# HGRN's eight projection blocks beside the forget ones as seven half products, with in-place quarter sums on GpSimd

## What is computed

```python
(hq, hf, hi, hg, gq, gk, gv, ga, gb, gz, gate_h, gate_g) = jnp.split(u @ w_in, offsets, axis=-1)
log_f = jnp.logaddexp(jnp.log(lb), jnp.log1p(-lb) + jax.nn.log_sigmoid(hf))
k_h = -jnp.expm1(log_f)
q_h = jax.nn.silu(hq) * HG_DK ** -0.5
o_h = hgrn2_chunked(q_h, k_h, hi, log_f)          # 8 heads of 128, chunks of 64
o_h = rmsnorm(o_h, hgrn_out_norm) * jax.nn.silu(hg)
y_h = o_h @ w_branch_hgrn
y = jax.nn.sigmoid(gate_h) * y_h + jax.nn.sigmoid(gate_g) * y_g
```

## Time and profile before

| | us |
|---|---|
| median of three runs | 2774.72 |
| lowest and highest | 2771.5, 2782.12 |
| profiled execution, whole | 2772.54 |
| its span | 2770.7 |
| from the start of hf to the start of y_h | 1189.6 to 1560.1 |

### The profile page before, as it was taken

The page is one execution under the profiler, slowest core; times in us unless marked ns, Lnnn a source line. Parts: engine busy times, 40 slices in busy tenths (PEclk is TensorE's granted clock), DMA queues, the critical chain, the costliest instruction groups (busy, mean ns, idle before and its releaser), DMA issues.

```text
span 2770.7 us, 29212 instructions
## 1 busy us (share of the span) xinstructions
PE 2708.6 (98%) x11644; PEld 1812.8 (65%) x11644; DVE 1260.6 (45%) x2499; ACT 638.8 (23%) x1460; POOL 59.6 (2%) x115
## 2 busy tenths in 40 slices
PE   8999899999999999999999999999999999999999
PEld 5445557656468888746556655656565685688886
DVE  3823333445234445526354426474655451344564
ACT  2122321246210000133342222424243202100001
POOL 0000000000000000000000001010110000000000
PEclk9999899999999999999999999999999999999999
DMA  4111011200122222211110130121111321222222
GB/s 157 61 61 58 25 57 66 91 31 1 61 64 89 91 92 91 77 61 61 61 61 31 63 122 31 61 77 40 68 46 61 145 91 61 91 92 85 74 86 76
DMA packets 122479, 195.17 MB, mean 70 GB/s; under 512 B 7212, under 2 KB 63336, under 8 KB 121448
## 3 DMA queue, kind: packets, MB, share of 16 engines
q1 hardware_dynamic: 120784, 181.15, 19.2%
q0 software_dynamic: 1296, 12.06, 1.1%
q10 hardware_dynamic: 264, 0.10, 0.0%
HBM read 185.95 MB, written 7.34 MB: 70 GB/s over the span
## 4 chain that ended last, share of the span: by engine, by line
PE 95%; DVE 2%; ACT 1%; DMA 1%; issue 1%; ACTq 0%; DVEq 0%; SPq 0%
PE psum L506 19%; PE psum L503 14%; PE psum L2239 14%; PE psum L416 9%; PE psum L436 8%; PE psum L2221 7%; PE psum L401 6%; PE psum L1141 2%; PE psum L2102 2%; PE psum L1161 2%; PE psum L634 1%; PE psum L389 1%; PE psum L1149 1%; PE psum L2450 1%; PE psum L2316 1%
## 5 line engine op out<-in xcount | busy, mean ns | idle before, releaser
L2239 PE MATMUL psum<-weight_ring,h_t 128*128 128x512 f32 x896 | 406.6, 596 | 0.5 <-issue 0.5
L559 DVE TENSOR_TENSOR arena<-arena,psum 128x512 f32<-128x512 f32 x179 | 122.9, 686 | 336.8 <-PE psum L506 287.6
L2239 PEld LDWEIGHTS psum<-weight_ring,h_t 128*128 128x128 f32 x896 | 162.0, 191 | 162.3 <-issue 161.1
L416 PE MATMUL psum<-h_t,weight_ring 128*128 128x512 f32 x560 | 245.7, 599 | 7.9 <-DMA weight_ring<-in_w_in_dram 4.2
L2221 PE MATMUL psum<-h_t,weight_ring 128*128 128x512 f32 x512 | 235.4, 601 | 1.7 <-ACT arena L2623 1.4
L506 PE MATMUL psum<-h_t,weight_ring 128*128 128x256 f32 x1024 | 228.2, 379 | 0.0
L503 PE MATMUL psum<-weight_ring,arena 128*128 128x256 f32 x992 | 220.2, 379 | 1.5 <-ACT arena L2660 1.5
L506 PEld LDWEIGHTS psum<-h_t,weight_ring 128*128 128x128 f32 x1024 | 194.5, 190 | 27.5 <-issue 1.3
L503 PEld LDWEIGHTS psum<-weight_ring,arena 128*128 128x128 f32 x992 | 188.4, 190 | 27.7 <-issue 2.2
L416 PEld LDWEIGHTS psum<-h_t,weight_ring 128*128 128x128 f32 x560 | 106.9, 192 | 142.3 <-issue 133.8
L401 PE MATMUL psum<-weight_ring,h_t 128*128 128x512 f32 (+3 forms) x512 | 182.1, 512 | 0.8 <-DVEq L1587 0.8
(11 more groups left out here) (396 smaller groups left out, 3288.6 us busy)
## 6 DMA issues: line engine op xcount, KB each, us to landing
weight_ring<-in_ffn_w_in_dram SPq DMA_DIRECT2D x44, 1024.0 KB, 7.3
weight_ring<-in_w_in_dram SPq DMA_DIRECT2D x20, 2048.0 KB, 7.8
weight_ring<-in_ffn_w_out_dram SPq DMA_DIRECT2D x8, 2048.0 KB, 8.0
weight_ring<-in_w_in_even_dram SPq DMA_DIRECT2D x7, 2048.0 KB, 8.1
weight_ring<-in_w_in_odd_dram SPq DMA_DIRECT2D x5, 2048.0 KB, 7.8
weight_ring<-in_w_in_dram SPq DMA_DIRECT2D x8, 1024.0 KB, 7.0
weight_ring<-in_w_branch_gdn_dram SPq DMA_DIRECT2D x4, 2048.0 KB, 7.9
weight_ring<-in_ffn_w_out_dram SPq DMA_DIRECT2D x4, 1536.0 KB, 6.7
```

The source lines that it names most:

```text
L416: last = pe.matmul(bank, slot[:, k, c:c + P], act[:, k, :], start=(k == 0), stop=(k == KD - 1))
L559: ins = dve.tensor_tensor(out, other, bank, op)
L2239: last = pe.matmul(bank, act[:, k, t * P:(t + 1) * P], slot[:, k, :], start=(k == 0), stop=(k == KD - 1))
```

## The change

Eight blocks, all but hf's, become seven half products each (`pe_seven_streamed`), in the order p4, p1, p2, p5, p6, p7, p3. It is a generator: `pe_take(stream, 1)` does one half product, 8 matmuls, so that they can stand between heads. The weights' sums are made by GpSimd in the ring itself (`pool_quarter_sums`): four operations of 128x1024 a block, the first after p4 has used the quarter that it overwrites, the third after p1, the fourth after p2; TensorE waits for the first at p5, for the third at p6, for the fourth at p3. The sums of the activations are made once, by VectorE, into the buffer of the residual `x_res`, which GpSimd's queue has written out to a scratch tensor in HBM and reads back after gate_h 1 (2 MB each way). Of a block's results ScalarE copies p4 (negated), p1 and p5, three operations of 128x512, and VectorE adds the rest in seven (`dve_streamed`). The activations Silu and Sigmoid, before taken from PSUM with the copy, are now applied to the finished blocks in SBUF. `HGRN_UNITS` says how many half products stand ahead of the first level and after each of them: 4, then 2, 2, 2, 2, 1, 1, 0 for half 0 and 6, then 2, 2, 2, 1, 1, 0, 0 for half 1.

```diff
+STREAMED = ("p4", "p1", "p2", "p5", "p6", "p7", "p3")
+def pe_seven_streamed(K, pe, key, act, tokens, token_major, among=None):
+    blk = K.next_block()
...
+    t1, t2, t4, t3 = sums_view(tokens, KD)
+    sides = {"p4": (w22, t4), "p1": (w11, x11), "p2": (w12, x21), "p5": (w22, t1), "p6": (w11, t2), "p7": (w21, t3),
+             "p3": (w12, x22)}
+    summed = {"p5": 1, "p6": 3, "p7": 3, "p3": 4}
...
+    for name in STREAMED:
...
+        if K.turn((key, name)) > 1:
+            pe.wait_ge(K.free_of((key, name)), K.turn((key, name)) - 1)
+        if name in summed:
+            pe.wait_ge(K.quarters_summed, at + summed[name])
...
+        yield
+def pool_quarter_sums(K, pool, key, blk):
+    w11, w12, w21, w22 = quarters(K, blk, KD)
+    pool.wait_ge(K.full_of((key, "p4")), K.turn((key, "p4")))
+    pool.tensor_tensor(w22, w21, w22, ALU.add).then_inc(K.quarters_summed, 1)
...
+    pool.tensor_tensor(w21, w11, w21, ALU.subtract).then_inc(K.quarters_summed, 1)
+    pool.wait_ge(K.full_of((key, "p1")), K.turn((key, "p1")))
...
+    pool.tensor_tensor(w11, w22, w11, ALU.subtract).then_inc(K.quarters_summed, 1)
+    pool.wait_ge(K.full_of((key, "p2")), K.turn((key, "p2")))
...
+    pool.tensor_tensor(w12, w12, w11, ALU.subtract).then_inc(K.quarters_summed, 1)
+def dve_streamed(K, dve, key, name, quarter, base, tmp):
...
+    if name == "p6":
+        dve_product(K, dve, key, "p6", base, base)
+        dve.wait_ge(K.free_of((key, "p5")), K.turn((key, "p5")))
+        dve.tensor_tensor(c12, pair(base), pair(tmp), ALU.add).then_inc(K.one_more("dve"), 1)
...
@@ pe_mix
+    K.token_sums["pe"] += 1
+    pe.wait_ge(K.tokens_summed, K.token_sums["pe"])
+    pe_take(pe_seven_streamed(K, pe, (s, "hq", 0), K.h_t, V["tokens_s"], False), 7)
     for g in range(2):
...
+        inner = pe_hgrn_stream(K, pe, s, V, g)
+        pe_take(inner, HGRN_UNITS[g][0])
...
+            pe_take(inner, HGRN_UNITS[g][1][lv])
...
-        pe_take(fill, 2 * KD)
+        pe_take(fill, 2)
         pe.wait_ge(K.phase_met, K.phase_end("pe"))
+        pe_take(fill, 2)
         pe_hgrn_states(K, pe, s, V, g, fill)
...
-            pe_take(fill, 2 * KD)
+            fill = pe_seven_streamed(K, pe, (s, "gate_h", 1), K.h_t, V["tokens_s"], True, FILL_BANKS)
+            pe_take(fill, 2)
         pe.wait_ge(K.phase_met, K.phase_end("pe"))
+    pe_take(fill, 2)
     pe.wait_ge(K.hgrn_gated, 2)
...
-    pe_take(fill, 2 * KD)
+    pe_take(fill, 3)
...
+HGRN_UNITS = ((4, (2, 2, 2, 2, 1, 1, 0)), (6, (2, 2, 2, 1, 1, 0, 0)))
...
@@ pe_hgrn_states
         if h == 3:
-            pe_take(fill, KD)
+            pe_take(fill, 2)
...
-    pe_take(fill, KD)
+    pe_take(fill, 1)
     pe.wait_ge(K.hgrn_states, g + 1)
...
@@ act_mix
+        part(beside, "p4")
+        part(beside, "p1")
         act.wait_ge(K.hgrn_to_end, g + 1)
...
@@ dve_mix
+    dve.wait_ge(K.x_spilled, 16)
+    dve_token_sums(K, dve, K.h_t, KD, V["tokens_s"])
...
+        dve.wait_ge(K.gates_open, g + 1)
         dve_head_norm(K, dve, V["o"], g * 512, 128, V["gate"], K.hgrn_squares, g + 1,
...
+    dve_hgrn_sums(K, dve, s, V, "gate_h", 1, ("p6", "p7"))
+    dve_weight_sums(K, dve, K.branch_blocks["y_h"], KD, V["weights0"], None)
+    dve_hgrn_sums(K, dve, s, V, "gate_h", 1, ("p3",))
+    dve_weight_sums(K, dve, K.branch_blocks["y_h"] + 1, KD, V["weights1"], None)
...
+def pool_hgrn(K, pool, s):
+    pool.wait_ge(K.lb_shifted, 1)
+    pool.dma_start(K.x_dram, K.x_res[:]).then_inc(K.x_spilled, 16)
+    for name, g in HGRN_ORDER:
+        pool_quarter_sums(K, pool, (s, name, g), K.streamed_at[(name, g)])
...
+    pool.dma_start(K.x_res[:], K.x_dram).then_inc(K.x_reloaded, 16)
```

More of the change, by code:

```diff
@@ L2531, in act_mix @@
         act.wait_ge(K.free_of((s, "o_t", kt)), K.turn((s, "o_t", kt)))
-    act_gate(K, act, V["gate_y"], (s, "gate_h", 1), 1, (2, 3))
+    for half in range(2):
+        last = ((s, "gate_h", half), "p3")
+        act.wait_ge(K.free_of(last), K.turn(last))
+        gate = V["gate_y"][:, :, half * BANK:(half + 1) * BANK]
+        act.activation(gate, gate, ACT.Sigmoid).then_inc(K.gates_open, 1)
     for half in range(2):
@@ L2906, in dve_mix @@
         dve_seven_fresh(K, dve, (s, "y_h", half), quarter, V["base"][:, 0, :])
[L2907 to L2908 removed]
+        dve.wait_ge(K.gates_open, 3 + half)
         y, gate = (V[name][:, :, half * BANK:(half + 1) * BANK] for name in ("y", "gate_y"))
```

163 lines of the change are left out of this document (112 added, 51 removed), and 3 rows, old and new, of the table HGRN_SUMS.

## The result

| | before | changed |
|---|---|---|
| median of twenty runs, us | 2777.02 | 2785.48 |
| lowest and highest, us | 2771.5, 2783.4 | 2775.01, 2798.34 |
| profiled execution, span, us | 2770.7 | 2779.6 |

The forecast of 2779 us had the sign and the class right; its sum gave +4.5 us.

What follows compares the result with a forecast made beforehand. TensorE alone was taken to bound the HGRN part. Saving -26.4, order's stalls +10.6 and clock +1.8 gave -14.0 us; GpSimd's holds with clock, +18.5, made +4.5: 2774.7 + 4.5 = 2779 us, range 2758 to 2797.

Steps and rivals of the forecast that it cites:

- The saving: TensorE's eight blocks as seven half products: 3.30 us saved a block, 26.4 us in all.
- Last meeting: End of the second half, at gate_h 1: thinner cover stalls TensorE 4.7 us; GpSimd's sums holding the norm add 6.6.
- start of the states: ScalarE's copies ahead of the table load make VectorE's product late: 1.5 us, twice, 3.0 in all.
- end of the states: VectorE needs 5.7 us to the signal, TensorE's cover shrinks to 1.7 + 3.45: 0.6 us, twice.
- tail of gate_h 1: After the transposes, TensorE waits at p3 (0.9 us) and ahead of y_h's first summed product (0.8): 1.7 us.
- The turns: GpSimd's sums push back VectorE's two-input SBUF work by 2.2 us each: 16.7 us together, 18.5 with clock.
- start of the second half: Four GpSimd sums fall into VectorE's scans and differences; after cover of 3.0, a stall of 4.6 us.
- its last levels: Second half's levels 5 and 6: hg's sums eat the lead at levels 3 and 4, costing 3.1 us.
- The clock: Half-rate matmuls behind a TensorE stall: 1.8 us for each stall of about 4 us, two such stalls.
- Rival C: VectorE keeps the port and GpSimd's sums starve: 2776 us, no change; chance 0.08.
- Rival B: A GpSimd sum is dearer than 2.2 us, each 1 us more costing 15: 2797 us at 3.4; chance 0.20.
- Rival A: GpSimd's sums don't hold VectorE, or only for moments: -14.0 us, 2761 us; chance 0.22.

Runs made afterwards that it cites:

- fifth run: Changed kernel with ScalarE's copy of p1 of the block beside moved behind the three activations and p5 given bank 5, sums still on GpSimd; ratio 1.0006.
- the first experiment: Changed kernel with GpSimd's 32 quarter sums cut to one column of 128x1, result wrong; ratio 0.996 to the kernel before.
- the best version: Changed kernel with quarter sums on VectorE, ScalarE's p1 copy behind the activations, four half products ahead of the last meeting; ratio 0.9929 to the kernel before.

## Why the prediction was right, and where it was off

**The saving.** Seven half products take 24.19 us (112 records, hq 0), as reckoned, 3.3 us less than a plain block.

**What the order costs.** The run with sums of one column measures it alone. Last meeting 4.59 against 4.7; start of the states 1.42 twice against 1.5 twice; end of the states 0.35 twice against 0.6 twice; tail of gate_h 1 0.70 and, behind the start of y_h, 0.36 against 1.7. Together 9.2 against 10.6. The spill landed in 8.1 us, 10.0 were assumed, and nobody waited for it.

**The turns.** GpSimd's sum alone 2.35 us against 2.2; what it takes from VectorE 1.9 to 2.2. Last meeting 10.92 - 4.59 = 6.3 against 6.6; start of the second half 4.68 against 4.6; its last levels 2.0 against 3.1; start of the first half 0.6 against 0.9; first end of the levels 3.18 - 1.42 = 1.8 against 1.5; not foreseen, the second one 0.3. Together 15.7 against 16.7. Both the form of the lock and its length were worked out from copies of 0.3 us, so this was the step that could have failed. Rival C falls: GpSimd waits 0.8 us behind operations of 1.2 us and at most 4.22 - 2.35 = 1.9 us (fifth run), behind one of 2.29, never longer than one operation of VectorE. Rival B falls: no sum costs VectorE more than 2.2. Rival A, that there is no hold, is what the first experiment built, and it came out at 0.996, 11 us below the kernel before (13.5 by the traces from hf to y_h), where A had 14.

**The clock.** This is the term of the sum that was mis-sized. I took 1.8 us for each of two stalls of over 4 us, 3.6 in all, from the one wait in the earlier trace rows. Measured were 10.0: 2.4 and 2.9 behind those two, and 4.7 behind the wait of 3.18 us, which I had left out because it is under 4. The price itself was read from a row that doesn't show it. In the kernel before the clock had fallen ahead of that wait, at 1612.5, while TensorE was busy all the time with 64 records of 128x32, and it stayed at half through them, the wait and the 3.6 us behind it:

```profile
1611.00:1612.00 1.00, 1.00 (x11) 1.00 (x10) 0.75 (x2) 0.00 (x0) 0.00 (x0) 1.00 1.02 346
1613.00:1618.00 5.00, 5.00 (x25) 5.00 (x24) 0.00 (x0) 0.18 (x1) 0.00 (x0) 0.50 1.05 374
```

So the earlier trace rows says nothing of what a stall that begins at full clock costs.

**The sum.** -26.4 + 24.5 of stalls (without the 0.36 that falls into y_h) + 10.0 of clock = +8.1 us; the trace has +10.5 from hf to y_h. The other 2.4 lie in gaps and starts of under 0.4 us that I did not trace one by one; the best version, with 0.7 + 0.5 of stalls and no half clock, also lies 1.3 above its sum of -25.2. Predicted were 27.3 of stalls and 3.6 of clock. The stalls were 2.8 too high and the clock 6.4 too low, and the rest makes the difference to +4.5. So that the forecast came as near as it did is in part luck: two errors of opposite sign. The time alone would not have told it from rival B either: at 2.6 us for each of GpSimd's sums, B gives +10.5 as well (4.5 + 0.4 x 15). Only the lengths in the traces tell them apart.

## What to carry to other kernels

Work given to GpSimd is free only where VectorE is idle or reads from PSUM: count each of its instructions on SBUF that meets VectorE's two-operand work as an instruction of VectorE of nearly the same length, and compare that with doing it on VectorE (here 2.1 against 1.23 us). When an engine's chain has become the bound, moving TensorE's work to where the stall shows mostly moves the stall; the chain has to get shorter or what holds it has to go elsewhere. And when a saving on TensorE thins the cover, list what stands ahead of every meeting and every first wait of a phase: two places of that kind, a copy ahead of a table load and two products ahead of a norm, cost 1.4 (twice) and 4.6 us even with nothing held, and let every hold through.
